# Sharing the split of the weights between GpSimd and VectorE in the SSD stretch of a two-layer trunk

## What is computed

```python
def ssd_mixer(h, w_in, conv_w, conv_b, dt_bias, a_log, d_skip, norm_g, w_out):
    zxbcdt = h @ w_in
    ...
    xbc = jax.nn.silu(causal_dwconv(xbc, conv_w, conv_b))
    ...
    y = ssd_scan(xs, dt, a, bm, cm)
    y = y + d_skip.astype(jnp.float32).reshape(N_GROUPS, HEADS_PER_GROUP)[..., None] * xs.astype(jnp.float32)
    y = y.reshape(b, s, D_INNER) * jax.nn.silu(z.astype(jnp.float32))
    yg = y.reshape(b, s, N_GROUPS, D_INNER // N_GROUPS)
    yg = yg * lax.rsqrt(jnp.mean(yg * yg, axis=-1, keepdims=True) + RMS_EPS)
    y = (yg.reshape(b, s, D_INNER) * norm_g.astype(jnp.float32)).astype(h.dtype)
    return y @ w_out
```

## Time and profile before

| | us |
|---|---|
| median of 3 runs | 1144.09 (1143.68 to 1145.13) |
| the profiled execution | 1145.98, its span 1144.2 |
| PE busy | 1110.4, 97% of the span |
| DVE busy | 556.3, 49% |
| POOL busy | 581.4, 51% |
| ACT busy | 464.7, 41% |
| `w_lo` on POOL, line 614 | 500.9 in 374 instructions, mean 1343 ns |

### The profile page before, as it was taken

How to read it: one execution, slowest core, us unless ns; L and a number is a source line. 1 busy time by engine, 2 the same in 40 slices (tenths; PEclk the granted TensorE clock), 3 DMA queues, 4 the chain that set the end, 5 groups by cost and what they waited for, 6 DMA issues and landing times.

```text
span 1144.2 us, 15307 instructions
## 1 busy us (share of the span) xinstructions
PE 1110.4 (97%) x5142; PEld 907.3 (79%) x5142; DVE 556.3 (49%) x655; ACT 464.7 (41%) x793; POOL 581.4 (51%) x440
## 2 busy tenths in 40 slices
PE   9999999999999999999899899799999999999996
PEld 6788888888888788787687787588888888888885
DVE  6656412465333473656747647334565214654123
ACT  7333222233233446575485567333332222333331
POOL 4666544444555545345263264445665444545661
PEclk9999999999999999999899999999999999999998
DMA  6322223222322234333313242123322232223221
GB/s 253 107 96 92 92 97 105 92 92 99 101 93 92 92 114 132 119 111 116 124 66 121 99 139 78 60 93 100 102 92 92 94 108 92 92 94 109 92 92 73
DMA packets 39428, 117.41 MB, mean 103 GB/s; under 512 B 4064, under 2 KB 10720, under 8 KB 39392
## 3 DMA queue, kind: packets, MB, share of 16 engines
q1 hardware_dynamic: 39104, 116.21, 30.2%
q10 hardware_dynamic: 288, 0.73, 0.2%
HBM read 114.70 MB, written 2.23 MB: 102 GB/s over the span
## 4 chain that ended last, share of the span: by engine, by line
PE 88%; DVE 6%; ACT 4%; issue 1%; POOL 1%; DMA 0%; DVEq 0%; ACTq 0%; POOLq 0%
PE bank L716 27%; PE bank L717 27%; PE bank L718 27%; PE bank L885 2%; PE bank L894 1%; DVE m L1177 1%; PE bank L902 1%; ACT m L540 1%; DVE x_conv L1096 1%; DVE act_lo L1233 1%; ACT w_hi L375 1%; PE bank L844 1%; PE bank L771 1%; DVE x_lo L967 0%; DMA x_token<-x_tok 0%
## 5 line engine op out<-in xcount | busy, mean ns | idle before, releaser
L614 POOL TENSOR_TENSOR w_lo<-w_raw,w_hi 128x512 fp32r<-128x512 f32 x374 | 500.9, 1343 | 508.2 <-ACT w_hi L375 508.0
L375 ACT ACTIVATE w_hi<-w_raw 128x512 fp32r<-128x512 f32 x374 | 233.9, 629 | 466.1 <-PE bank L718 465.2
L716 PE MATMUL bank<-x_hi,w_hi 128*128 128x512 f32 x856 | 339.3, 396 | 2.6 <-DVE x_lo L967 1.7
L717 PE MATMUL bank<-x_lo,w_hi 128*128 128x512 f32 x856 | 333.6, 390 | 0.0
L718 PE MATMUL bank<-x_hi,w_lo 128*128 128x512 f32 x856 | 333.6, 390 | 0.0
L716 PE MATMUL bank<-act_hi,w_hi 128*128 128x512 f32 x640 | 252.9, 395 | 0.6 <-DVE act_lo L1233 0.6
L717 PE MATMUL bank<-act_lo,w_hi 128*128 128x512 f32 x640 | 249.2, 389 | 0.0
L718 PE MATMUL bank<-act_hi,w_lo 128*128 128x512 f32 x640 | 249.2, 389 | 0.0
L716 PEld LDWEIGHTS bank<-x_hi,w_hi 128*128 128x128 f32 x856 | 161.0, 188 | 39.5 <-issue 5.0
L717 PEld LDWEIGHTS bank<-x_lo,w_hi 128*128 128x128 f32 x856 | 161.0, 188 | 34.9 <-issue 2.4
L718 PEld LDWEIGHTS bank<-x_hi,w_lo 128*128 128x128 f32 x856 | 160.9, 188 | 33.7
(11 more groups left out here) (130 smaller groups left out, 654.1 us busy)
## 6 DMA issues: line engine op xcount, KB each, us to landing
w_raw<-weights SPq DMA_DIRECT2D x187, 512.0 KB, 3.3
m<-acs_scratch SPq DMA_DIRECT2D x16, 512.0 KB, 4.5
decay_in<-eacs_scratch SPq DMA_DIRECT2D x24, 128.0 KB, 3.6
x_token<-x_tok SPq DMA_DIRECT2D x4, 512.0 KB, 6.7
residual<-xt SPq DMA_DIRECT2D x8, 256.0 KB, 9.9
out_t<-scaled_residual SPq DMA_DIRECT2D x8, 256.0 KB, 2.4
pooling_matrices<-pooling ACTq DMA_DIRECT2D x1, 576.0 KB, 5.3
constants<-consts SPq DMA_DIRECT2D x1, 192.0 KB, 10.2
```

Of the source, the lines that this page charges most:

```text
L375: act.activation(whi[:, c % 2, part], raw[:, c % 2, part], ACT.Copy).then_inc(hi_ready, 1)
L614: pool.tensor_tensor(wlo[:, c % 2, part], raw[:, c % 2, part], whi_f[:, c % 2, part], ALU.subtract).then_inc(lo_ready, 1)
L716: pe.matmul(out, wh, xh, start=start, stop=False)
L717: pe.matmul(out, wh, xl, start=False, stop=False)
```

## The change

In the units whose weights are made ready during the SSD stretch (`V_FROM` = unit 68 up to `V_TO` = `U_MLP1`, unit 123: 55 units) POOL subtracts the first half only. The second half is subtracted by DVE, in a new function `ahead(u)`, called in every slot behind `conv_scale`, `gate_in` or `add_output` and ahead of all else of the slot that stands behind these. It waits for ACT's second half and counts a semaphore of its own, `lo_v_ready`. TensorE waits for this at the second half of a unit, and SP waits for both counts before a load.

```diff
--- before.py
+++ after.py
@@ -39,6 +39,9 @@
 A_SSM = A_MLP0 + 48
 A_OUT = A_SSM + 1 + 4 * PER_GROUP
 A_MLP1 = A_OUT + 16
+
+
+V_FROM, V_TO = U_SSM + 2, U_MLP1
 
 
 COLS = {}
@@ -178,6 +181,7 @@
         raw_landed = [sem("raw_landed0"), sem("raw_landed1")]
         hi_ready = sem("w_hi_ready")
         lo_ready = sem("w_lo_ready")
+        lo_v_ready = sem("w_lo_vector_ready")
         wt_used = sem("w_used")
         acc_drained = sem("acc_drained")
         pool_added = sem("pool_added")
@@ -261,7 +265,11 @@
 
         def lo_source(c, half, r=0):
 
-            return lo_ready, 2 * c + half + 1 + 2 * r
+            if V_FROM <= c < V_TO:
+                if half:
+                    return lo_v_ready, c - V_FROM + 1
+                return lo_ready, c + V_FROM + 1
+            return lo_ready, 2 * c - (V_TO - V_FROM if c >= V_TO else 0) + half + 1 + 2 * r
 
         def conv_out(n):
 
@@ -276,6 +284,8 @@
             def load_weights(c, r=0):
 
                 if c >= 2:
+                    if V_FROM <= c - 2 < V_TO:
+                        sp.wait_ge(*lo_source(c - 2, 0))
                     sp.wait_ge(*lo_source(c - 2, 1, r))
                 sp.dma_start(raw[:, c % 2, :], weights[bass.ds(c + r, 1), :, :].rearrange("a p n -> (a p) n")
                              ).then_inc(raw_landed[c % 2], 16)
@@ -607,7 +617,7 @@
         def _(pool):
             def split_half(c, half, r=0):
 
-                if isinstance(r, int) and c + r >= UNITS:
+                if isinstance(r, int) and (c + r >= UNITS or half and V_FROM <= c < V_TO):
                     return
                 pool.wait_ge(hi_ready, 2 * c + half + 1 + 2 * r)
                 part = slice(512 * half, 512 * half + 512)
@@ -1076,6 +1086,15 @@
             mlp(U_MLP0, A_MLP0, 0, 0, 2)
 
 
+            def ahead(u):
+
+                c = U_SSM + u + 2
+                if c >= V_TO:
+                    return
+                dve.wait_ge(hi_ready, 2 * c + 2)
+                dve.tensor_tensor(wlo[:, c % 2, 512:], raw[:, c % 2, 512:], whi_f[:, c % 2, 512:],
+                                  ALU.subtract).then_inc(lo_v_ready, 1)
+
             def unit_done(u):
                 dve.wait_ge(wt_used, 2 * (U_SSM + u + 1))
 
@@ -1103,9 +1122,11 @@
             invert(1, rstd, 1)
             dve.wait_ge(recip_done, 2)
             dve.tensor_tensor(tmp[:, 0, :], acc3[0][:, :], rstd[:, :], ALU.mult).then_inc(acc_drained, 1)
+            ahead(0)
 
             dve.wait_ge(consts_landed, 16)
             conv_scale(0)
+            ahead(1)
             conv_taps(0)
             dve.wait_ge(dtt_ready, 1)
             dt_bias = col("dt_bias", 0, HEADS).unsqueeze(1).to_broadcast(hd4)
@@ -1115,6 +1136,7 @@
                                      op0=ALU.mult, op1=ALU.min).then_inc(dt_na, 1)
             link(dve.tensor_scalar(mx[:, :, :], dtx[:, :, :], 0.0, None, ALU.max))
             conv_scale(1)
+            ahead(2)
             conv_taps(1)
             dve.wait_ge(dt_exp, 2)
             link(dve.tensor_scalar(rc[:, :, :], ex[:, :, :], 2.0, None, ALU.add))
@@ -1140,6 +1162,7 @@
                     dve.tensor_tensor(dend[:, :], cum[:, 1, :], acs, ALU.subtract).then_inc(dend_in, 1)
                     dve.tensor_copy(acs_f[:, :], b_yd[0:HEADS, :]).then_inc(acsf_ready, 1)
                 conv_scale(u - 1)
+                ahead(u)
                 conv_taps(u - 1)
 
             def by_head(ap):
@@ -1299,6 +1323,7 @@
                             norm_lo(g, i)
             for m in range(KD):
                 add_output(KD + m)
+                ahead(slot_of(GROUPS - 1, GT + 8 + m))
                 residue(3, m)
 
             mlp(U_MLP1, A_MLP1, 32, 6, None)
```

## The result

The changed kernel takes 1146.44 us (median of 20 executions, 1143.74 to 1150.81), the kernel before 1144.11 measured beside it (20 executions, 1141.03 to 1146.28). The ratio is 1.0024, with an interval from 1.0013 to 1.0035: 2.7 us slower, where 0.5 us faster was forecast. The profiled execution of the changed kernel took 1145.94 us and has a span of 1144.1. That is no more than the 1145.98 and 1144.2 of the execution of the kernel before from which the forecast was made; but that one stood 1.9 us above its kernel's median.

What follows compares the result with a forecast made beforehand. TensorE, busy for 97% of the span, was taken as the bound, so only its idles and clock falls mattered. Terms 0.1 - 2.14 - 2.1 + 1.65 + 1.7 + 1.0 - 0.7 = -0.5 us gave 1143.6 us, range 1140.4 to 1146.4.

Steps and rivals of the forecast that it cites:

- slot 9, two idles shortened: Chunk 3 of groups 1 and 2: without POOL's contention `m` ends 1.07 us earlier, twice; -2.14 us.
- clock at these two: Chunk 3 of groups 1 and 2: shorter idles may keep TensorE's clock; half of 4.16 us taken, -2.1 us.
- slot 2 of groups 1 to 3: Chunk 0's `m` stands behind DVE's subtraction and POOL's `x_dt_decayed`; new idle of 0.55 us three times, +1.65 us.
- slot 6 of group 3: DVE's subtraction waits for ACT, delaying `norm_y` and chunk 3's `m`; new idle 2.25 us, 0.55 recovered, net +1.7 us.
- clock at slot 6: Group 3's new idle before chunk 3 may drop TensorE's clock; half of a mean 2.1 us, +1.0 us.
- slot 11 of group 3: TensorE's 0.63 us wait for `act_lo`, which shared time with POOL's second half, goes; -0.7 us with small gaps.
- convolution slots, loads: Subtraction fits DVE's gap behind `conv_scale`, 0.1 us for group 0's chunk 3; loads cost nothing, estimated bound 1 us.
- The two gains: Chunk 3 of groups 1 and 2: shorter idles, -2.14 us, and clock kept there, -2.1 us.
- 0 (something else holds it): Lower bound on the gain at each chunk 3 idle of groups 1 and 2; upper bound 1.07 us each.
- the second rival: Clock falls at idles from 2.0 us on, at chunk 3 of groups 1 to 3; +2.7 us, 1146.8, chance 0.15.
- The two added waits: New TensorE idles: 0.55 us ahead of chunk 0 of groups 1 to 3, 2.25 us ahead of group 3's chunk 3.
- The 0.85 us gap behind `conv_scale`: DVE idles there until ACT's first tap; the subtraction takes 0.72 us of it, at no cost.

Runs made afterwards that it cites:

- e4: Kernel before with only three subtractions on DVE, the second halves of slot 9 of groups 0 to 2; ratio 0.9997 (0.9987 to 1.0007).
- the second execution: Profiled execution from a rerun of the kernel before with no edit; ratio of that rerun 0.9991 (0.9979 to 1.0003).
- e5: Kernel before with a small memset ahead of chunk 3's `m` in groups 1 and 2, so POOL's second half always goes first; ratio 1.0025 (1.0005 to 1.0045).
- e10: Kernel before with its four 2.05 us idles ahead of chunks 2 and 3 lengthened by memsets to 3.34 and 3.14 us; ratio 1.0040 (1.0028 to 1.0052).
- e6: Kernel before with `m` of chunk 2 at the head of slot 6 and of chunk 3 behind `conv_scale` in slot 8, groups 0 to 2; ratio 0.9905.
- the first four experiments: Follow-up runs, among them the kernel before rerun with no edit (ratio 0.9991), beside which 33 executions of the kernel before were measured.
- e8: Changed kernel, one subtraction back on POOL, `m` of chunks 0 to 3 and the last group's square root moved earlier; 1124.14 us, ratio 0.9833 to kernel before.

## Why the prediction was wrong

The forecast was 1143.6 us, 0.5 less than before, in a range to 1146.4; it came out at 2.7 more by the ratio, which is 1146.8 on the same median. By the parts of the sum:

| part | predicted | measured |
|---|---|---|
| slot 9, two idles shortened | -2.14 | 0 (e4) |
| clock at these two | -2.1 | 0 (e4) |
| slot 2 of groups 1 to 3 | +1.65 | +1.1 (0.35, 0.37, 0.39) |
| slot 6 of group 3 | +1.7 | +1.4 (2.17, less 0.77 at the statistic) |
| clock at slot 6 | +1.0 | about +0.9 over the whole kernel |
| slot 11 of group 3 | -0.7 | -0.6 |
| convolution slots, loads | +0.1 | 0 |
| sum | -0.5 | +2.8 |

**The step that failed is the first of the gains, slot 9, and the clock that hung on it.** I took the 2.29 us `m` of the earlier trace rows for what this kernel does. It was what it did in one execution, in which POOL came 0.05 us ahead. The two gains, 4.24 us of the sum, belonged to that execution, which at 1145.98 us was already 1.9 above the median of 1144.09, and I took them off the median. The rows had a warning that I didn't read: both instructions were released by different chains and started 0.05 us apart, so which came first was open, and 3.14 in both groups looked like a rule only because both come from the same execution and the same order of events. The trace of the second execution has 2.06 and 2.05, e4 shows that taking the race away gives nothing, and e5 that losing it always costs 2.9 us. The bound "0 (something else holds it)" was in the text, but as an outlying case.

**The clock terms.** From three rows (kept after 2.04, lost after 2.27 and 2.74) I took it to be likely enough that 2.07 would keep the clock to book half of 4.16 us. In the changed kernel's trace it fell after 2.04 (547.32), and held after 2.05 (564.91). Over the 13 traces the four idles of about 2.04 us stand 28 times, and 14 times a fall begins about the idle's end or up to 1.4 us behind it. Whether it falls after 2 us is a matter of the single execution, as the second rival had it, and these idles paid for it all along. In the traces a fall came with each of the 21 idles of over 3 us as well, but not in every execution: the fastest of e5, with its two of 3.14 us, has a mean clock of 0.994, which beside the 5 us at the program's end leaves room for about one fall. So shortening 3.14 to 2.05 would have spared little (e10), while a new idle of 2.17 costs its share.

**What held.** The two added waits came where and as the order and the rows had them, each a little smaller than worked out: `m` in slot 2 was held up as described but ended at 516.96, not 517.4, since everything ran 0.25 us earlier and the second `x_dt_decayed` was done sooner. The 2.17 us in slot 6 was forecast at 2.25. The 0.85 us gap behind `conv_scale` did cover the subtraction: `w_lo` on DVE takes 0.69 us at the median, and in no slot did TensorE wait for it (shortest, median and longest of the 55, in ns):

```profile
L1095 DVE TENSOR_TENSOR w_lo<-w_raw,w_hi x55: 669/693/1365, 392.1 to 770.0; 128x512 fp32r<-128x512 f32 x55
```

The second rival (no gain of clock, a new fall, 1146.8) is nearest to what happened, and it got 0.15. It was right about the clock. That its number is met so closely is luck in part: the waits it counted as shortened, 2.14 us, weren't there in most executions, and it put the other waits and the new fall too high by about as much.

What stays open is the split of the last 0.9 us of clock: the mean clocks are given to three digits, and executions of one kernel differ by more than the change makes.

## What to carry to other kernels

Before a contention in a trace is booked as a gain, look at how far apart the two instructions started and what released each; if it is a few hundredths of a microsecond, the next execution may have them the other way round, and a second profile of the same kernel costs less than a wrong sum. When work is moved to another engine, what counts is not its length but the instruction that it waits for: four of 55 moved subtractions (at two kinds of place) stood behind a late ACT result and ahead of something that TensorE needed, and they alone turned a gain of 2 us into a loss of 3. The waits that were there all along were worth 10.9 us (e6), five times that gain, and moving `m` into gaps in which DVE idled removed them.

## What was not expected of the hardware

- Two instructions that hold each other up and start 0.03 us apart were not served in the order of their records: at 561.85 POOL and 561.88 DVE, DVE went first and POOL took 2.39 us in place of 1.3; with 561.92 and 561.97 POOL went first.
- TensorE's clock fell after idles of 2.04 us in one place and not after 2.05 in another of the same execution.
- The loss comes in steps. Each fall in the SSD stretch of the 13 traces lasts 3.4 us or twice that, and so costs about 1.7 or 3.4 us. The kernel before agrees in its times: the 33 executions measured with the first four experiments stand in heaps near 1141.0, 1142.5, 1144.1, 1145.6 and 1146.3 us, with mean clocks of 0.992, 0.991, 0.989 to 0.990, 0.988 and 0.987, while span times clock stays within 1129.1 to 1131.6 us. With most idles gone (e8) the four executions lie within 1.6 us, though four are few.
